# Moving the weight ring and the stationary buffers to other SBUF addresses, in a float32r decoder layer whose matmuls split each operand in two

## The reference, cut to what matters

```python
D_MODEL = 2048; SEQ = 256; D_FF = 5632; N_MEM = 256; XA_HEADS = 4

h = h + 0.5 * _swiglu(_rmsnorm(h, g_ffn1[l]), w_ffn1_in[l], w_ffn1_out[l])
z = _rmsnorm(h, g_mix[l]) @ w_mix_in[l]
gate_b, gate_c, h_c, u, v = jnp.split(z, splits, axis=-1)
y_conv = gate_b * _causal_dwconv(gate_c * h_c, conv_w[l], conv_b[l])
y_gm = _spatial_gating(u, v, g_gm_v[l], w_spatial[l], b_spatial[l])
h = h + jnp.concatenate([y_conv, y_gm], axis=-1) @ w_mix_out[l]
h = h + _cross_attention(_rmsnorm(h, g_xattn[l]), _rmsnorm(mem, g_mem[l]),
                         w_xq[l], w_xk[l], w_xv[l], w_xo[l])
h = h + 0.5 * _swiglu(_rmsnorm(h, g_ffn2[l]), w_ffn2_in[l], w_ffn2_out[l])
return _rmsnorm(h, g_final)
```

## Time and profile before

| | us |
|---|---|
| time, median of 2 runs | 2189.39 |
| the two runs | 2189.5 and 2189.28 |
| span of the profiled execution, first to last instruction | 2187.2 |
| TensorE matmul busy in it | 2167.1 |
| VectorE busy | 1349.3 |
| ScalarE busy | 991.6 |

### The profile page before, as it was taken

The page is one execution under the profiler, slowest core; times in us unless marked ns, Lnnn a source line. Parts: engine busy times, 40 slices in busy tenths (PEclk is TensorE's granted clock), DMA queues, the critical chain, the costliest instruction groups (busy, mean ns, idle before and its releaser), DMA issues.

```text
span 2187.2 us, 25558 instructions
## 1 busy us (share of the span) xinstructions
PE 2167.1 (99%) x9626; PEld 1778.9 (81%) x9626; DVE 1349.3 (62%) x1549; ACT 991.6 (45%) x1103; POOL 1.8 (0%) x7
## 2 busy tenths in 40 slices
PE   8999999999999999999999999999999999999998
PEld 6888888888888888888888888888888888888886
DVE  5676667666474547865677554576676667664544
ACT  5444454444343444444554444454444444443433
POOL 0000000000000000000000000000000000000000
PEclk9999999999999999999999999999999999999999
DMA  6666666665556565665556445466666666665553
GB/s 227 209 190 197 195 191 188 197 195 189 188 171 204 181 191 181 195 227 175 180 170 207 155 159 169 157 212 197 193 191 193 192 192 190 195 194 187 188 188 135
DMA packets 159217, 412.20 MB, mean 188 GB/s; under 512 B 12588, under 2 KB 13732, under 8 KB 158756
## 3 DMA queue, kind: packets, MB, share of 16 engines
q1 hardware_dynamic: 157728, 410.04, 60.2%
q10 hardware_dynamic: 1412, 1.11, 0.2%
HBM read 409.01 MB, written 2.10 MB: 188 GB/s over the span
## 4 chain that ended last, share of the span: by engine, by line
PE 96%; DVE 2%; ACT 1%; DMA 0%; issue 0%; ACTq 0%; DVEq 0%
PE ps L906 94%; PE ps L935 1%; DVE w_lo L575 1%; PE ps L919 1%; DVE ps L635 1%; DVE convT L748 0%; DVE xT_lo L583 0%; DMA h<-in_x 0%; ACT convT L444 0%; PE ps L1023 0%; ACT xT_hi L329 0%; ACT w_hi L321 0%; DVE stage L738 0%; ACT scratch L555 0%; ACT zT L441 0%
## 5 line engine op out<-in xcount | busy, mean ns | idle before, releaser
L575 DVE TENSOR_TENSOR w_lo<-raw,w_hi 128x1024 fp32r<-128x1024 f32 x768 | 936.1, 1224 | 773.8 <-ACT w_hi L321 768.6
L321 ACT ACTIVATE w_hi<-raw 128x1024 fp32r<-128x1024 f32 x768 | 811.8, 1061 | 1106.0 <-PE ps L906 1087.0
L906 PE MATMUL ps<-w_hi,xT_hi 128*128 128x512 f32 x1856 | 573.8, 390 | 5.3 <-DVE w_lo L575 5.3
L906 PE MATMUL ps<-w_lo,xT_hi 128*128 128x512 f32 x1856 | 572.2, 389 | 0.0
L906 PE MATMUL ps<-w_hi,xT_lo 128*128 128x512 f32 x1856 | 572.0, 389 | 0.0
L906 PEld LDWEIGHTS ps<-w_hi,xT_hi 128*128 128x128 f32 x1856 | 347.8, 188 | 78.9 <-issue 4.1
L906 PEld LDWEIGHTS ps<-w_lo,xT_hi 128*128 128x128 f32 x1856 | 349.0, 188 | 72.7
L906 PEld LDWEIGHTS ps<-w_hi,xT_lo 128*128 128x128 f32 x1856 | 348.7, 188 | 72.8
L906 PE MATMUL ps<-w_hi,hidT_hi 128*128 128x512 f32 x704 | 223.5, 397 | 0.4 <-DVE w_lo L575 0.4
L906 PE MATMUL ps<-w_hi,hidT_lo 128*128 128x512 f32 x704 | 222.7, 395 | 0.0
L906 PE MATMUL ps<-w_lo,hidT_hi 128*128 128x512 f32 x704 | 221.3, 393 | 0.0
(11 more groups left out here) (119 smaller groups left out, 800.7 us busy)
## 6 DMA issues: line engine op xcount, KB each, us to landing
raw<-in_w_ffn_in SPq DMA_DIRECT2D x352, 512.0 KB, 4.1
raw<-in_w_ffn_out SPq DMA_DIRECT2D x176, 512.0 KB, 4.3
raw<-in_w_mix_in SPq DMA_DIRECT2D x80, 512.0 KB, 4.2
raw<-in_w_mix_out SPq DMA_DIRECT2D x32, 512.0 KB, 3.7
raw<-in_w_xq SPq DMA_DIRECT2D x32, 512.0 KB, 3.8
raw<-in_w_xk SPq DMA_DIRECT2D x32, 512.0 KB, 3.9
raw<-in_w_xv SPq DMA_DIRECT2D x32, 512.0 KB, 3.6
raw<-in_w_xo SPq DMA_DIRECT2D x32, 512.0 KB, 3.6
```

What stands on the lines that cost most here:

```text
L321: nc.scalar.activation(w_hi[:, k % RING, :], raw[:, k % RAW, :], ACT.Copy).then_inc(hi_ready, 1)
L575: nc.vector.tensor_tensor(w_lo[:, k % RING, :], raw[:, k % RAW, :], w_hi[:, k % RING, :].bitcast(F32), ALU.subtract).then_inc(lo_ready, 1)
L906: ins = nc.tensor.matmul(bank(s, t * GW + b * BLK, BLK), xs[:, k, t * P:(t + 1) * P], ws_[:, k % RING, b * BLK:(b + 1) * BLK], start=(k == ...
```

## The change

Three things are moved, and no instruction is added or removed. The first tensor after `h` starts at 0 modulo 256. The ring slots of `w_hi` and `w_lo` are 4112 bytes apart in place of 4096, so that slots 0 to 3 start at 0, 16, 32 and 48 modulo 256. And `hidT` starts at 64, `yT` at 128, `memT` and all that shares its region at 192 modulo 256.

```diff
+    PITCH = 256
     place = {"at": BASE}
+
+    def lane(at, to):
+        return at + (to - at) % PITCH
...
     h = put("h", [P, TOK, D], F32)
+    place["at"] = lane(place["at"], 0)
     xT_hi = put("xT_hi", [P, KD, SEQ], F32R)
     xT_lo = put("xT_lo", [P, KD, SEQ], F32R)
     raw = put("raw", [P, RAW, GW], F32)
-    w_hi = put("w_hi", [P, RING, GW], F32R)
-    w_lo = put("w_lo", [P, RING, GW], F32R)
+    SKEW = 4
+    SLOT = GW + SKEW
+    place["at"] = lane(place["at"], 0)
+    w_hi_ring = put("w_hi", [P, RING * SLOT], F32R)
+    place["at"] = lane(place["at"], 0)
+    w_lo_ring = put("w_lo", [P, RING * SLOT], F32R)
+    w_hi = [w_hi_ring[:, i * SLOT:i * SLOT + GW] for i in range(RING)]
+    w_lo = [w_lo_ring[:, i * SLOT:i * SLOT + GW] for i in range(RING)]
...
-    big = extra + 8 * KB
+    big = lane(extra + 8 * KB, 64)
     hidT_hi = put("hidT_hi", [P, KF, SEQ], F32R, at=big)
     hidT_lo = put("hidT_lo", [P, KF, SEQ], F32R, at=big + KF * KB)
-    yT_hi = put("yT_hi", [P, KD, SEQ], F32R, at=big)
-    yT_lo = put("yT_lo", [P, KD, SEQ], F32R, at=big + 16 * KB)
-    memT_hi = put("memT_hi", [P, KD, SEQ], F32R, at=big + 32 * KB)
-    memT_lo = put("memT_lo", [P, KD, SEQ], F32R, at=big + 48 * KB)
+    yT_hi = put("yT_hi", [P, KD, SEQ], F32R, at=big + 64)
+    yT_lo = put("yT_lo", [P, KD, SEQ], F32R, at=big + 64 + 16 * KB)
+    memT_hi = put("memT_hi", [P, KD, SEQ], F32R, at=big + 128 + 32 * KB)
+    memT_lo = put("memT_lo", [P, KD, SEQ], F32R, at=big + 128 + 48 * KB)
...
-                    nc.scalar.activation(w_hi[:, k % RING, :], raw[:, k % RAW, :], ACT.Copy).then_inc(hi_ready, 1)
+                    nc.scalar.activation(w_hi[k % RING], raw[:, k % RAW, :], ACT.Copy).then_inc(hi_ready, 1)
...
-                    nc.vector.tensor_tensor(w_lo[:, k % RING, :], raw[:, k % RAW, :], w_hi[:, k % RING, :].bitcast(F32),
+                    nc.vector.tensor_tensor(w_lo[k % RING], raw[:, k % RAW, :], w_hi[k % RING].bitcast(F32),
                                             ALU.subtract).then_inc(lo_ready, 1)
...
-                                                       ws_[:, k % RING, b * BLK:(b + 1) * BLK],
+                                                       ws_[k % RING][:, b * BLK:(b + 1) * BLK],
```

More of the change, by code:

```diff
@@ L142, in build @@
     g_fin = put("g_fin", [P, D], F32, at=extra)
-    big = extra + 8 * KB
+    big = lane(extra + 8 * KB, 64)
     hidT_hi = put("hidT_hi", [P, KF, SEQ], F32R, at=big)
     hidT_lo = put("hidT_lo", [P, KF, SEQ], F32R, at=big + KF * KB)
-    yT_hi = put("yT_hi", [P, KD, SEQ], F32R, at=big)
-    yT_lo = put("yT_lo", [P, KD, SEQ], F32R, at=big + 16 * KB)
-    memT_hi = put("memT_hi", [P, KD, SEQ], F32R, at=big + 32 * KB)
-    memT_lo = put("memT_lo", [P, KD, SEQ], F32R, at=big + 48 * KB)
[L150 to L159, removed]
+    yT_hi = put("yT_hi", [P, KD, SEQ], F32R, at=big + 64)
+    yT_lo = put("yT_lo", [P, KD, SEQ], F32R, at=big + 64 + 16 * KB)
+    memT_hi = put("memT_hi", [P, KD, SEQ], F32R, at=big + 128 + 32 * KB)
+    memT_lo = put("memT_lo", [P, KD, SEQ], F32R, at=big + 128 + 48 * KB)
+    c_buf = put("c_buf", [P, TOK, GW], F32, at=big + 128 + 32 * KB)
+    zT = put("zT", [P, HALF, SEQ], F32, at=big + 128 + 40 * KB)
+    convT = put("convT", [P, HALF, SEQ], F32, at=big + 128 + 48 * KB)
+    v_buf = put("v_buf", [P, TOK, GW], F32, at=big + 128 + 56 * KB)
+    wsT = put("wsT", [P, HEADS, P], F32, at=big + 128 + 64 * KB)
+    sg = put("sg", [P, TOK, GW], F32, at=big + 128 + 80 * KB)
+    mem_nat = put("mem_nat", [P, TOK, D], F32, at=big + 128 + 64 * KB)
+    v_hi = put("v_hi", [P, TOK, GW], F32R, at=big + 128 + 64 * KB)
+    v_lo = put("v_lo", [P, TOK, GW], F32R, at=big + 128 + 72 * KB)
+    pT_lo = put("pT_lo", [P, XA_HEADS * 2, SEQ], F32R, at=big + 128 + 80 * KB)
     qT_hi, qT_lo = yT_hi, yT_lo
     kT_hi, kT_lo = xT_hi, xT_lo
-    assert big + 2 * KF * KB <= nc.sbuf_usable_end
+    assert big + 128 + 2 * KF * KB <= nc.sbuf_usable_end
     vectors = [("g_ffn1", g_ffn1[0], KD), ("g_mix", g_mix[0], KD), ("g_xattn", g_xattn[0], KD), ("g_mem", g_mem[0], KD),
```

## The result

| | before | after |
|---|---|---|
| time, median of 2 runs each, us | 2189.39 | 2213.28 (2212.6 and 2213.97) |
| span of the profiled execution, us | 2187.2 | 2212.2 |

The ratio is 1.0108 with a 95% interval of 1.0089 to 1.0127: the change makes the kernel 1.1% slower. The interval doesn't contain 1, so the kernel did become slower. The difference lies inside the prediction's 2% and on the forecast side, and it is more than twice the forecast size (24 us in place of 11).

What follows compares the result with a forecast made beforehand. TensorE's stream was taken as the bound; `xT` +21.2 us and the others -10.2 us sum to +11.0 us, making the span 2198.2 and, with 2.2 us around it, 2200.4, forecast as 2200 us, range 2163 to 2229.

Steps and rivals of the forecast that it cites:

- the prediction's 2%: Whole kernel: what a measurement can tell from no change, 44 us; a result within it had chance 0.83.
- The bound and what decides: TensorE's stream: busy 2167.1 of 2187.2 us; the matmul step decides, each nanosecond on all 9216 being 9.2 us.
- the price of the unseen distances: Ring matmuls: 230.5 ns at every stage, giving `xT` +21.2 us, the others -10.2 us, sum +11.0 us.
- the unsettled value: Ring matmuls: the 230 and 231 ns of phases not yet settled, held likeliest since each distance lasts only 12 matmuls.
- The sign of being wrong that the prediction named: Ring matmuls: a price of the 15 unseen distances outside 226.7 to 233.3 ns would above all make it wrong.
- Only distance 0 is good: Ring matmuls: all other distances settle at 233.3 ns; 2226 us, or 2217 us if slot 0 keeps 226.7; chance 0.20.
- The alignment of the stationary operand: Stationary buffers: multiples of 64 bytes make all matmuls 226.7 ns, gaining 24.1 us, to 2165 us; chance 0.12.
- free distances: Ring matmuls: some distances come near the bare 213.3 ns; 2121 us at half of them, 2161 at a quarter; chance 0.09.
- distances worse than 160: Ring matmuls: half the distances cost another 6.7 ns, 240, and half 233.3; 2257 us; chance 0.10.
- Addresses don't matter: Ring matmuls: the change does nothing, something else about the buffer makes `xT` faster; 2189 us; chance 0.10.
- The smaller terms: Outside the ring matmuls: ScalarE and VectorE means unchanged and covered by idle time, DMA 0 us.
- L935's bound: Score and value matmuls: 192 at up to 6.7 ns either way, 1.3 us at the most, put at 0.

Runs made afterwards that it cites:

- e1: Kernel before, with ring and all four stationary buffers at 0 modulo 256, so every ring matmul has distance 0: 2165.95 us.
- e2: Kernel before, with ring and all four stationary buffers at 32 modulo 256, so distance 0 everywhere: 2167.18 us.
- e8: Kernel before, with distances held for good: `xT` at 8, `hidT` at 40, `yT` at 168, `memT` at 232: 2248.57 us.
- e5: Kernel before, with distances held for good: `xT` at 240, `hidT` at 16, `yT` at 48, `memT` at 80: 2212.79 us.
- e11: Kernel before, with the ring at 16 and all stationary buffers at 32 modulo 256, so distance 16 everywhere: 2230.86 us.
- e9: Kernel before, with distances held for good: `xT` at 248, `hidT` at 24, `yT` at 152, `memT` at 216: 2220.75 us.
- e6: Kernel before, with distances held for good: `xT` at 224, `hidT` at 32, `yT` at 96, `memT` at 160: 2225.61 us.
- e3: Kernel before with only the buffers' part of the change: `hidT` at 64, `yT` at 128, `memT` at 192, ring step still 4096 bytes: 2184.46 us.
- e7: Kernel before, with distances held for good: `xT` at 208, `hidT` at 112, `yT` at 144, `memT` at 176: 2219.66 us.

## Why the prediction was right or wrong

**The bound and what decides** were right: TensorE's stream, the step from start to start, and through it the addresses of the operands. The whole difference lies in the ring matmuls. By the rule of the Trainium skill (TensorE: Matmul & The Clock Gate, Step-by-step: what each phase is for), that loading a stationary tile takes no read bandwidth from the running matmul, no address would matter. The trace doesn't agree: moving nothing but addresses took the steady step from 226.7 to 240.0 ns. Whether it is the reads that collide, no trace shows.

**The step that failed** is the price of the unseen distances. I took 230.5 ns, "the unsettled value", because each distance lasts for only 12 matmuls. The measured means are 232.0 (`xT`), 232.0 (`hidT`), 233.3 (`yT`), 231.4 (`memT`). By the prediction's own sum:

- `xT`: 5568 x (232.0 - 226.7) = +29.5 us, where I had +21.2.
- the others: 2112 x (232.0 - 233.3) + 768 x (231.4 - 233.3) = -4.2 us, where I had -10.2.
- Sum +25.3 us; the span grew by 25.0.

For distance 0, the only one that rows 6 and 7 had shown unsettled, the price was right: 230.3 ns. For the others it was taken over without a row.

The reasoning behind it was wrong too, not the number alone. I had read the 230 and 231 ns after a change of stage as an average that any disturbed stream has. They are the way back to a good phase that distance 0 has and most distances don't. Held for good, the distances of the change take the steps in this table, and but for distances 0 and 16 the changed kernel's slots took the same ones within 1.1 ns. The numbers are means over the starts in the trace, so most are the mean of a repeated pattern. The sign of being wrong that the prediction named, a price outside 226.7 to 233.3 ns, came true in single slots: 234.9 ns for `hidT` at 48, 234.3 for `memT` at 160. Besides, the unseen distances were 14 and not 15: the 16 of the change without 0 and 160. Of `xT`'s 29.5 us, the three quarters of its matmuls that had the distances 240, 224 and 208 account for 1392 x (4.8 + 7.0 + 6.0) = 24.8 us, and the interrupted distance 0 for 1392 x 3.6 = 5.0 us.

```
distance held     ns per matmul of 512 columns     kernel
  0               226.7                            e1, e2
  8               236.6                            e8
 16               226.7, 233.3 or 236.7            e5, e11
 24               233.3                            e9
 32               233.3                            e6
 40               233.4                            e8
 48               230.0 or 234.6                   e5
 64               233.3                            e3
 80               233.3 (one short stretch 230.9)  e5
 96               234.2                            e6
112               233.3                            e7
128               232.4                            e3
144               231.2 (one stretch 226.7)        e7
152               233.3                            e9
160               233.3                            before, e6
168               240.0 (238.8 with the way there) e8
176               231.1                            e7
192               229.0                            e3
208               233.3 (short stretches 230.0)    e7
216               235.0                            e9
224               233.3                            e6
232               234.6 to 235.0                   e8
240               231.7                            e5
248               232.1, 232.5 or 233.3            e9
```

**The rivals.** "Only distance 0 is good" (0.20, 2217 or 2226 us) was nearest: its mechanism is what the table shows, and the mean over the new distances did pass the 229.3 ns from which it decides (232.1); 16 and 192 took the edge off. The alignment of the stationary operand (0.12) fell with e2_all_same_32; free distances (0.09) were not found among 24; distances worse than 160 do exist: off the multiples of 16 there are 8, 168, 216 and 232, and 168 has just the 240 ns that this rival had assumed; at multiples of 16, which are all that the change uses, only 48 and 96 by about 1 ns and 16 in one of its phases. "Addresses don't matter" (0.10) is refuted.

**The smaller terms** held: ScalarE and VectorE unchanged and covered, DMA of no effect (its share in `xT`'s stretch 0.64 against 0.65). L935's bound held as well: by the starts, each of its four groups of 48 matmuls took 5.66 to 5.69 us after and 5.74 to 5.75 before, together 0.3 us.

**The range** reached to 2229 and held the time, and the sign was right because `xT` has most of the matmuls and had the most to lose. What was wrong is the size: 11 us forecast, 24 measured.

## What to carry to other kernels

Where TensorE streams float32r at 2.4 GHz with a stationary load per matmul, read the step from start to start by stage and compare it with columns / 2.4 ns; if stages of one shape differ, look at the addresses of their operands. Try the same address modulo 256 for the moving and the stationary operand, ring and all stationary buffers alike, and no skew between slots: in this kernel that is worth 1.1% (2165.95 against 2189.36 us, e1_all_same) for a rounding in the allocator. Don't price an address that no row shows by how a stream recovers elsewhere; hold each for a whole stage and measure it.

## What the runs showed of the hardware that was not expected

- A float32r matmul of 512 columns never had a steady step below 226.7 ns, 13.3 ns over its bare stream of 213.3, at any of 24 distances. Why that remainder exists, and what collides, stays open: the trace shows starts, not stalls, and two read streams in conflict is my reading, not shown.
- One distance can have several steady steps, and which one holds depends on what ran before. At 16 bytes the FFN output products of the two FFNs ran at 236.7 and 226.7 ns in one execution, for over 200 us each; at 144, 192 matmuls in a row (40 us from 1002 us of e7_steady_c) ran at the good step and the neighbouring stretches at 231.2. What in the work before picks the step stays open. Stretch of e7_steady_c with `yT` at 144, 40.39 / 178 = 226.9 ns:

```profile
1002.00:1042.00 40.00, 40.00 (x178) 33.13 (x177) 1.00 0.50 162
```

- The price depends on the length as well. The 48 score matmuls of 256 columns take 5.75 us at distance 160 and at distance 0, but less at distance 64, where 512 columns cost 233.3 ns. Scores of one pair, e1_all_same (distance 0):

```profile
1207.83:1213.58 5.75, 5.75 (x48) 5.70 (x47) 1.00 0.58 186
```

and e5_steady_a (distance 64), 114.0 ns each against 119.8:

```profile
1239.23:1244.70 5.47, 5.47 (x48) 5.43 (x47) 1.00 0.59 190
```
